# Two pieces of padding in a float32r transformer kernel: where the activations of the output products begin in SBUF

## What is computed

```python
h = rmsnorm(x, norm_pre_mix)                    # block one
m = hgrn2_mixer(h, hgrn_w_in, hgrn_w_out, ...)  # 2048 -> 10240, recurrences, then o @ w_out
x = x + rmsnorm(m, norm_post_mix)
up = dwconv3(rmsnorm(x, norm_pre_ffn) @ ffn_w_in, ffn_w_conv)      # 2048 -> 11264
x = x + rmsnorm((silu(gate) * val) @ ffn_w_out, norm_post_ffn)     # 5632 -> 2048
x = x + mixed @ w_out_2                         # block two: attention and delta rule, then 2048 -> 2048
x = x + memory_cross_attention(...)             # ends in @ w_xo_2, 512 -> 2048
x = x + conv_ffn_2(...)                         # ends in @ w_down_2, 5632 -> 2048
return rmsnorm_2(x, final_norm)
```

## The kernel before, in words

| tile | role in a product | before | after the change |
|---|---|---|---|
| `wts`, `x`, `raw` | loaded (narrow) or streamed (wide, token) | 128 | 128 |
| `hs`, `memr`, `m`, `hold` | streamed (narrow), loaded (token) | 288 | 288 |
| `os_`, `mixs`, `xs`, `acts` | loaded (wide) | 288 | 128 |
| `mems` | streamed (narrow), loaded (token) | 288 | 288 (moved by 512) |
| `hin`, `KQ`, `KM`, `ones_r`, `sqh`, `sql`, `AD`, `AO` | small products of the recurrence | 288 | 128 |
| `sums_r`, `gb_rows` | small products | 128 | 480 |
| `sin`, `spp`, `gy`, `TT`, `Z`, `Tm` and their neighbours | small products | 160 | 0 |
| `cst` (identity, ones) | small products | 480 | 480 |

## Time and profile before

### The profile page before, as it was taken

One profiled execution on the slowest core, in us unless ns is written; L12 is line 12 of the kernel. 1 busy time (PEld: TensorE's weight loads), 2 busy tenths in 40 slices (PEclk: granted clock), 3 DMA queues, 4 the chain that ended last, 5 costly groups with the idle time before them and its releaser, 6 DMA issues.

```text
span 2695.2 us, 47424 instructions
## 1 busy us (share of the span) xinstructions
PE 2683.5 (100%) x17616; PEld 2291.9 (85%) x17616; DVE 1971.6 (73%) x2721; ACT 1335.3 (50%) x1679; POOL 133.9 (5%) x138
## 2 busy tenths in 40 slices
PE   9999999999999999999999999999999999999998
PEld 8888888888888888888888888878888888888887
DVE  6888888878888888644466677767678888885444
ACT  6455555455444444433465566665644444443443
POOL 0211121210000000000000000000000000000000
PEclk9999999999999999999999999999999999999999
DMA  7555555475555555655645544355455555556554
GB/s 245 180 165 172 165 168 173 161 196 170 189 187 187 187 187 187 195 187 187 218 139 181 170 145 139 134 171 186 150 190 187 187 187 187 187 188 197 185 184 150
DMA packets 136197, 481.68 MB, mean 179 GB/s; under 512 B 14880, under 2 KB 19120, under 8 KB 135680
## 3 DMA queue, kind: packets, MB, share of 16 engines
q1 hardware_dynamic: 134160, 472.06, 53.2%
q0 software_dynamic: 1376, 7.46, 0.8%
q10 hardware_dynamic: 528, 0.26, 0.0%
HBM read 477.63 MB, written 2.10 MB: 178 GB/s over the span
## 4 chain that ended last, share of the span: by engine, by line
PE 82%; DVE 8%; issue 4%; DMA 3%; ACT 2%; DVEq 1%; SPq 0%; ACTq 0%
PE acc L442 29%; PE acc L444 15%; PE acc L465 8%; PE acc L467 8%; PE acc L466 8%; PE acc L414 4%; DMA raw<-stream 3%; DVE wts L362 3%; PE acc L415 2%; ACT wts L355 2%; DVE cy L2313 2%; DVE cin L392 1%; DVE half L380 1%; PE ps L1406 1%; PE ps L740 1%
## 5 line engine op out<-in xcount | busy, mean ns | idle before, releaser
L442 PE MATMUL acc<-hs,wts 128*128 128x512 f32 x4640 | 1626.8, 394 | 0.0
L362 DVE TENSOR_TENSOR wts<-raw,wts 128x1024 fp32r<-128x1024 f32 x888 | 1061.9, 1227 | 525.0 <-ACT wts L355 524.3
L355 ACT ACTIVATE wts<-raw 128x1024 fp32r<-128x1024 f32 x888 | 913.6, 1055 | 847.0 <-PE acc L444 367.9
L444 PE MATMUL acc<-hs,wts 128*128 128x256 f32 x4640 | 1297.1, 280 | 0.0
L442 PEld LDWEIGHTS acc<-hs,wts 128*128 128x128 f32 x4640 | 871.0, 188 | 194.1 <-DVE wts L362 0.9
L444 PEld LDWEIGHTS acc<-hs,wts 128*128 128x128 f32 x4640 | 871.5, 188 | 0.5
L467 PE MATMUL acc<-wts,acts 128*128 128x512 f32 x688 | 272.8, 396 | 0.0
L465 PE MATMUL acc<-wts,acts 128*128 128x512 f32 x688 | 272.6, 396 | 0.2 <-DVE wts L362 0.2
L466 PE MATMUL acc<-wts,acts 128*128 128x512 f32 x688 | 270.4, 393 | 0.0
L369 ACT ACTIVATE half<-acc 128x512 f32<-128x512 f32 x161 | 95.3, 592 | 157.7 <-PE acc L444 138.9
L466 PEld LDWEIGHTS acc<-wts,acts 128*128 128x128 f32 x688 | 129.2, 188 | 32.2
(11 more groups left out here) (361 smaller groups left out, 2172.7 us busy)
## 6 DMA issues: line engine op xcount, KB each, us to landing
raw<-stream SPq DMA_DIRECT2D x888, 512.0 KB, 4.1
xf<-xT SPq DMA_DIRECT2D x8, 256.0 KB, 6.6
raw<-stream SPq DMA_DIRECT2D x8, 256.0 KB, 6.7
fm<-memT POOLq DMA_DIRECT2D x2, 1024.0 KB, 6.6
fw<-stream POOLq DMA_DIRECT2D x2, 1024.0 KB, 10.7
memr<-memT POOLq DMA_DIRECT2D x1, 2048.0 KB, 9.8
outT<-memr SPq DMA_DIRECT2D x7, 256.0 KB, 2.8
KQ<-masks POOLq DMA_DIRECT2D x1, 448.0 KB, 5.7
```

Of the source, the lines that this page charges most:

```text
L355: nc.scalar.activation(high, source, ACT.Copy).then_inc(hi_ready, 1)
L362: nc.vector.tensor_tensor(low, source, high.bitcast(F32), ALU.subtract).then_inc(lo_ready, 1)
L442: nc.tensor.matmul(acc[:, 2 * par + n, :], whi[:, b, c:c + P], src[:, kt, :], start=start, stop=False)
L444: mm = nc.tensor.matmul(acc[:, 2 * par + n, 0:T], wlo[:, b, c:c + P], src[:, kt, 0:T], start=False, stop=stop)
```

## The change

88 float32 columns (352 bytes) are allocated, and never used, right after `hold`; as they are held by the outer context, all tiles declared after them move up by 352 bytes. The unused tile below `mems` grows by 40 float32 (160 bytes), so `mems` and the two tiles above it move by 512. No instruction is added, removed or put elsewhere.

```diff
         hold = sb("hold", [P, DT, 2 * T])
+        sb("to_weights", [P, 88])
         with ExitStack() as st:
             fw = sb("fw", [P, 2, BLK], F32, st)
...
         with ExitStack() as st:
-            sb("below_mems", [P, DT, 2 * T], F32, st)
+            sb("below_mems", [P, DT * 2 * T + 40], F32, st)
             mems = sb("mems", [P, DT, 2 * T], F32R, st)
```

## The result

The changed kernel takes 2679.77 us (median of four runs, 2679.31 to 2681.40) against 2696.88 us for the kernel before, measured beside it; the ratio is 0.9936, with a 95% interval of 0.9923 to 0.9948. That is 17.1 us less. The forecast was 9.8 us less, and its range ended at 2684.0 us. The profiled execution of the changed kernel took 2680.03 us.

The account below looks back on a forecast made before the run. TensorE's matmul spacing was taken to bound the kernel: 2976 wide matmuls x 3.3 ns = 9.8 us, all else zero, so 2697.01 - 9.8 = 2687.2 us profiled, 2686.8 us for the median; range 2684.0 to 2693.0 us.

Parts of the forecast that it names:

- What bounds the kernel: Whole kernel: TensorE, busy for all of the span at 2.4 GHz, is bound by how fast one matmul starts after another.
- the size of the gain per wide matmul: Wide products: 3.3 ns cheaper for each of 2976 matmuls, 9.8 us in all.
- The three comparisons behind it: Wide matmuls against narrow ones (3.0 ns), token against narrow pairs (3.1 ns), wide against L1710 (4.0 ns).
- The mechanism: 512-column streams: a load beginning 32 bytes off a multiple of 64 slows the spacing; a load from 128 is faster.
- rival C: Wide products: the 3 ns belong to the shape, not the address, so no gain; 2696.6 us, within 1 us; 15%.
- its 3.1 ns: Token pairs, 350.0 ns against 346.9 for narrow pairs, taken as the price of a load from 288 (`mems`).
- One sign that the forecast named: Two small groups change places: L1466 (`ones_r` now at 128) down from 397, L1710 (`sums_r` now at 480) up from 391.
- Rival D: Wide products: load and stream both starting at 128 get in each other's way, +9.8 us, 2706.4 us; 6%.
- The zero for the small products, VectorE, ScalarE, DMA and `mems`: Recurrence matmuls on moved tiles, other engines' work, loads, and `mems` kept at offset 288: no change in time.
- The refill of the ring: Weight ring: refill needs 3.4 us while the other pair of slots lasts 5.5 us, so some 2 us in hand.

Follow-up runs that it names:

- ring_160_acts_160: Kernel before with pads placing the ring `wts` at 160, `hs` at 352, `mems` at 288 and the wide products' activations at 160; 2709.1 us.
- acts_320: Changed kernel with the wide products' activations beginning at 320, `hs` and `mems` at 288, the ring `wts` at 128; 2685.6 us.
- ring_160: Kernel before with pads placing the ring `wts` at 160, `hs` at 352, `mems` at 288 and the wide products' activations at 128; 2725.0 us.
- ring_192: Kernel before with pads placing the ring `wts` at 192, `hs` at 352, `mems` at 288 and the wide products' activations at 128; 2686.2 us.
- order_changed: Changed kernel with each narrow output half's matmuls reordered, four of 512 columns first, then four of 256, instead of taking turns; same places; 2707.0 us.
- hs_128: Kernel before with one 352-byte pad ahead of `hs` instead of the change's two; `hs`, `hold`, wide activations, `mems` and ring at 128; 2705.9 us, ratio 1.0029.

## Why the prediction was wrong, point by point

**What bounds the kernel** held: TensorE's spacing, and no other engine. The change took time from the wide products, and from nothing else to speak of.

**The term that failed is the size of the gain per wide matmul.** The forecast said 3.3 ns, "between them and nearer to the two that rest on hundreds of matmuls or on dense stretches". It was 20 / 3 = 6.67 ns. The three comparisons behind it took for well placed what only was better placed or differently cut. The drawn 392 ns of a narrow 512-column matmul was read as its cost, 230.3 ns. But in a pair that takes turns the start of the 256-column matmul is not where the 512 columns' share ends; only the pair's sum means something. The sum was there to be read: 346.7 ns is 768 columns at 2.4 GHz, 320.0 ns, and 2 x 13.3 ns. The same 13.3 ns on top of 512 columns gives 226.7 ns, the very spacing that the wide products now have, and 6.6 ns less than the 233.3 of the earlier trace rows. With that the term would have been 2976 x 6.67 = 19.8 us, against a measured 17.1. The rest stayed in the short runs of `mixs` and `os_`, whose matmuls don't reach the dense pace, and in the new waits; the sum had a term for neither.

**The mechanism was half right.** That addresses set the pace, and not the shape alone (rival C), is shown by the padding runs: the same wide triples took from 680 to 703 ns. That the loaded tile's own place does it, 32 bytes off a multiple of 64, is refuted. ring_160_acts_160 loads from 160, 32 off such a multiple, and has the full gain; acts_320 is on a multiple and had 686.7 ns; ring_160 spoiled the wide products without touching the place they load from. The token pairs, which gave the prediction its 3.1 ns, didn't owe it to the place of the load either: in ring_192 those on `mems` load from 288 as before and take 346.8 ns.

One sign that the forecast named did come out, by luck. L1466 and L1710, L1467 and L1711 now, were to change places, and about did:

```profile
L1467 PE MATMUL ps<-sql,ones_r x8: 389/391/397, 140.5 to 564.6; 128*128 128x512 f32 x8
```
```profile
L1711 PE MATMUL ps<-spp,sums_r x8: 390/394/398, 1412.5 to 1524.0; 128*128 128x512 f32 x8
```

L1467 fell from 397 to 391 and L1711 rose from 391 to 394. But in both groups the loaded and the streamed tile had moved by the same 352 bytes, so their own distance is what it was, and L1466, which loads `ones_r` as well, kept its median of 396. order_changed has these tiles in the same places as the changed kernel and differs only in the order of the narrow matmuls around them. There the same two lines read:

```profile
L1469 PE MATMUL ps<-sql,ones_r x8: 388/388/397, 141.9 to 570.1; 128*128 128x512 f32 x8
```
```profile
L1713 PE MATMUL ps<-spp,sums_r x8: 389/390/392, 1428.1 to 1540.4; 128*128 128x512 f32 x8
```

The neighbours alone moved L1711 back from 394 to 390 and the other from 391 to 388, half the difference and more that the earlier trace rows were read for. Eight matmuls between other products don't isolate the place of their load; they should have carried less weight.

**Rival C** would have given 2696.6 us. With it goes the rule from the Trainium skill, "SBUF — State Buffer", sections "Door 1: The DMA port swizzle" (lines of 16 bytes) and "Who interferes with whom" (independent ports for the streamed operand and for the load). By it none of these placements should differ. All offsets here are multiples of 32, and triples ran from 680 to 703 ns; the traces don't agree.

**Rival D**, slower because load and stream begin at the same offset, named a real thing at the wrong spot. At distance 0 the wide products are at their best, but most narrow pairs of hs_128 lose 6.7 ns. That kernel takes 26 us more than the changed one and is slower than the one before.

**The zero for the small products, VectorE, ScalarE, DMA and `mems`** held: their phases moved by tenths of a microsecond, and busy VectorE time by 0.1 us.

**The refill of the ring** was given "some 2 us in hand" from a stretch with nothing beside it. In `os_`, where VectorE has the recurrence too, there was no such margin, and TensorE's matmuls were held up there by 0.6 us more.

## What to carry to other kernels

When a matmul stream is dense, compare its start-to-start time with its columns at the granted clock, over whole repeating units, and look at what is left per matmul; a difference between two kinds of product in that rest is a lead worth 0.6% here. If it is there, shift one of the two tiles by pads of 32 bytes and read the spacing from one profiled run each. What counted here was the distance between the tile that is loaded and the one that is streamed. Expect the gain in long dense stretches, and little of it where small products break the stream every few matmuls. A pad moves everything behind it, so work out the distance for every product: one pad of the same size 32 KiB earlier turned this gain of 17 us into a loss of 8.

## What the runs showed of the hardware that was not expected

- For float32r products with 128 loaded columns, a dense stream's pace depends on the distance between loaded and streamed tile. For the wide products it is the same for distances that differ by 256 bytes, in all placements tried: 680 ns at 0 and 256, 686.7 at 192 and -64, 700 at 224 and -32. The narrow pairs have 346.7 at 96 and at -160.
- The best pace comes to the same in both kinds of product, the columns at 2.4 GHz and 13.3 ns per matmul: 3 x 226.7 = 680 and 226.7 + 120.0 = 346.7 ns. No placement went below it.
- The wide products reach it at 0 alone; 512 and 256 columns taking turns reach it at 96 and 224. The order of the lengths has a part in this, and whether it is all of it is open. The curve isn't symmetric: 192 gives 686.7 ns, 64 gives 700.
- At distance 0 and at 32 the same pairs on the same tiles run at 353.3 ns in some stretches and at 346.7 in others of the same run. What sets which of the two a stretch takes wasn't found.
- It made no difference whether the weights or the activations are loaded. Narrow and token pairs have the same time at the same distance (96: 346.7 both; 160: 350.0 both). What inside the memory or the array makes this pattern stays open; the runs show only the times.
